# Gate and up projections of the second block: 512 weight columns moving against activations held, and the product turned by TensorE

## The reference, cut to what matters

```python
# x: (1, 256, 2048); h: (1, 256, 2048)
h = rms_norm_2(x, g_pre_ffn[l]) * (1.0 + scale_f) + shift_f
# w_ffn_gate, w_ffn_up: (2048, 5632); w_ffn_down: (5632, 2048)
f = (jax.nn.silu(h @ w_ffn_gate[l]) * (h @ w_ffn_up[l])) @ w_ffn_down[l]
x = x + gate_f * rms_norm_2(f, g_post_ffn[l])
```

## Time and profile before

| | |
|---|---|
| median of three runs | 2501.56 us |
| lowest and highest | 2496.78, 2502.04 us |
| profiled execution, its own time | 2500.57 us |
| its span in the profile | 2498.7 us |
| mean granted TensorE clock | 0.965 of full speed |
| PE busy | 2359.4 us (94%) |
| DVE busy | 1603.2 us (64%) |
| ACT busy | 1109.9 us (44%) |
| DMA | 502.02 MB, mean 201 GB/s |

### The profile page before, as it was taken

How to read it: one execution, slowest core, us unless ns; L and a number is a source line. 1 busy time by engine, 2 the same in 40 slices (tenths; PEclk the granted TensorE clock), 3 DMA queues, 4 the chain that set the end, 5 groups by cost and what they waited for, 6 DMA issues and landing times.

```text
span 2498.7 us, 37713 instructions
## 1 busy us (share of the span) xinstructions
PE 2359.4 (94%) x15624; PEld 2121.9 (85%) x15624; DVE 1603.2 (64%) x2266; ACT 1109.9 (44%) x1725; POOL 23.3 (1%) x59
## 2 busy tenths in 40 slices
PE   6989899899999999999979999996999999999997
PEld 5879777689998899998858787675999988999985
DVE  3996656678887778888765464646555555545444
ACT  3423566444444334444445464544434444444442
POOL 0000000000000000000000000000000000000000
PEclk9989989989999999999989899997999999999998
DMA  7745412668888888888854453252666667655552
GB/s 184 245 138 168 131 51 76 219 211 276 277 275 285 310 279 279 272 287 290 297 166 147 146 186 109 85 173 102 212 225 214 226 232 222 222 177 186 186 193 76
DMA packets 137770, 502.02 MB, mean 201 GB/s; under 512 B 15312, under 2 KB 15312, under 8 KB 137344
## 3 DMA queue, kind: packets, MB, share of 16 engines
q1 hardware_dynamic: 136368, 494.37, 58.6%
q0 software_dynamic: 1232, 5.24, 1.3%
HBM read 494.31 MB, written 5.24 MB: 200 GB/s over the span
## 4 chain that ended last, share of the span: by engine, by line
PE 84%; DVE 10%; ACT 3%; DMA 1%; issue 1%; POOL 1%; SPq 0%; ACTq 0%; DVEq 0%
PE bank L573 77%; DVE conv_y L1535 3%; DVE w_lo L1462 3%; PE bank L722 1%; DMA raw<-weights 1%; PE bank L757 1%; PE bank L545 1%; ACT w_hi L1034 1%; PE bank L610 0%; PE bank L739 0%; DVE wide L1480 0%; PE bank L622 0%; PE bank L752 0%; DVE x L1994 0%; DVE wide L1992 0%
## 5 line engine op out<-in xcount | busy, mean ns | idle before, releaser
L1462 DVE TENSOR_TENSOR w_lo<-raw,w_hi 128x1024 fp32r<-128x1024 f32 x737 | 888.0, 1220 | 550.6 <-ACT w_hi L1034 550.3
L573 PE MATMUL bank<-h_hi,w_hi 128*128 128x256 f32 x3472 | 993.7, 286 | 21.0 <-DVE w_lo L1462 20.6
L1034 ACT ACTIVATE w_hi<-raw 128x1024 fp32r<-128x1024 f32 x737 | 759.8, 1052 | 522.2 <-PE bank L573 503.4
L573 PE MATMUL bank<-h_lo,w_hi 128*128 128x256 f32 x3472 | 986.9, 284 | 0.0
L573 PE MATMUL bank<-h_hi,w_lo 128*128 128x256 f32 x3472 | 986.7, 284 | 0.0
L573 PEld LDWEIGHTS bank<-h_hi,w_hi 128*128 128x128 f32 x3472 | 670.1, 193 | 31.8 <-DVE w_lo L1462 30.9
L573 PEld LDWEIGHTS bank<-h_lo,w_hi 128*128 128x128 f32 x3472 | 670.4, 193 | 0.1
L573 PEld LDWEIGHTS bank<-h_hi,w_lo 128*128 128x128 f32 x3472 | 669.9, 193 | 0.0
L573 PE MATMUL bank<-w_hi,ff_hi 128*128 128x512 f32 x704 | 276.0, 392 | 2.9 <-DVE w_lo L1462 2.9
L573 PE MATMUL bank<-w_lo,ff_hi 128*128 128x512 f32 x704 | 274.0, 389 | 0.0
L573 PE MATMUL bank<-w_hi,ff_lo 128*128 128x512 f32 x704 | 274.0, 389 | 0.0
(11 more groups left out here) (293 smaller groups left out, 1818.1 us busy)
## 6 DMA issues: line engine op xcount, KB each, us to landing
raw<-weights SPq DMA_DIRECT2D x924, 512.0 KB, 4.4
bias_rows<-table POOLq DMA_DIRECT2D x1, 3072.0 KB, 35.5
raw<-weights SPq DMA_DIRECT2D x5, 504.0 KB, 3.4
x<-x SPq DMA_DIRECT2D x2, 1024.0 KB, 5.8
bias<-bias_rows POOLq DMA_DIRECT2D x1, 2048.0 KB, 17.1
out<-x SPq DMA_DIRECT2D x8, 256.0 KB, 2.0
lasting<-params SPq DMA_DIRECT2D x1, 550.0 KB, 7.7
raw<-weights SPq DMA_DIRECT2D x1, 488.0 KB, 3.2
```

The lines of the kernel that those rows point to most:

```text
L573: t = e.matmul(out, s, m, start=opens and first and q == 0, stop=closes and last and q == 2)
L1034: e.activation(w_hi[:, n % PART_SLOTS, 0:widths[i]], raw[:, i % RAW_SLOTS, 0:widths[i]], ACT.Copy).then_inc(hi_ready, 1)
L1462: e.tensor_tensor(w_lo[:, slot, 0:widths[i]], raw[:, i % RAW_SLOTS, 0:widths[i]], w_hi[:, slot, 0:widths[i]].bitcast(F32), ALU.subtract).t ...
```

## The change

Gate and up of the second block go from the tile form to the group form. The 22 tiles of a half become six groups: five of 512 columns and one of 256. The product is then tokens on partitions; it is held in one buffer `product` of 2 x 512 columns, and TensorE transposes it 128 x 128 at a time into banks 6 and 7, two feature tiles (a "pair", one bank) together. ScalarE rounds the turned pair from the bank into `ff_hi`, VectorE makes `ff_lo` from the bank. The transposes of a group are put behind the first weight chunk of the next gate group, or, for the last group of a half, behind the first chunk of the first down group. The order of the weights in memory follows the plan; the number of weight chunks and of ada chunks stays. The diff below has, in this order, the plan and the buffer, then TensorE's program, ScalarE's and VectorE's.

```diff
+FF_GROUPS = [[(6 * half + g, P * FF_HALF * half + 512 * g, min(512, P * FF_HALF - 512 * g)) for g in range(6)] for half in range(2)]
...
-        for j in range(FF_HALF * half, FF_HALF * (half + 1)):
-            p.project(("gate", j), "w_ffn_gate", P * j, P)
-            p.project(("up", j), "w_ffn_up", P * j, P)
+        for g, col, n in FF_GROUPS[half]:
+            p.project(("gate", g), "w_ffn_gate", col, n)
+            p.project(("up", g), "w_ffn_up", col, n)
...
-        sw_g = place("sw_g", FR, 2048, [P, 2, T])
+        product = place("product", FR, 2048, [P, TT, 512])
...
+        def ff_pairs(g):
+            half, at_group = divmod(g, 6)
+            return range(11 * half + 2 * at_group, min(11 * half + 2 * at_group + 2, 11 * (half + 1)))
...
+            def turn_product(g):
+                for pair in ff_pairs(g):
+                    b = 6 + pair % 2
+                    fill(b)
+                    for at_tile in range(2):
+                        col = (2 * (pair - ff_pairs(g)[0]) + at_tile) * P
+                        for tt in range(TT):
+                            w.wait_ge(ffn_product, FF_TILES + 2 * g + tt + 1)
+                            t = e.transpose(banks[b][:, at_tile * T + tt * P:at_tile * T + (tt + 1) * P], product[:, tt, col:col + P], identity)
+                    t.then_inc(ff_turned, 1)
+                    free[b] = ff_ready, FF_TILES + pair + 1
...
-                    tile(("gate", j), h_hi, h_lo, need, (ffn_silu, FF_TILES + j + 1))
-                    tile(("up", j), h_hi, h_lo, need, (ffn_product, FF_TILES + j + 1))
+                for g, col, n in FF_GROUPS[half]:
+                    gating = group_steps(("gate", g), n, (0, 1), h_hi, h_lo, need)
+                    next(gating)
+                    if g % 6:
+                        turn_product(g - 1)
+                    whole(gating)
+                    free[0], free[1] = (ffn_silu, FF_TILES + 2 * g + 1), (ffn_silu, FF_TILES + 2 * g + 2)
+                    group(("up", g), n, (2, 3), h_hi, h_lo, need)
+                    free[2], free[3] = (ffn_product, FF_TILES + 2 * g + 1), (ffn_product, FF_TILES + 2 * g + 2)
+                ff_need = lambda k, half=half: w.wait_ge(ff_ready, FF_TILES + 11 * half + k // 2 + 1)
...
+                    down = group_steps(("down2", half, n), 512, pair, ff_hi, ff_lo, ff_need)
+                    next(down)
+                    if n == 0:
+                        turn_product(6 * half + 5)
+                    whole(down)
...
+            def ff_round(g, first_chunk):
+                round_until(first_chunk + AHEAD)
+                for pair in ff_pairs(g):
+                    w.wait_ge(ff_turned, pair + 1)
+                    jj = 2 * (pair % 11)
+                    e.activation(ff_hi[:, jj:jj + 2, :].rearrange("p a t -> p (a t)"), banks[6 + pair % 2][:, :], ACT.Copy).then_inc(ff_rounded, 1)
...
+                for g, col, n in FF_GROUPS[half]:
+                    if g % 6:
+                        ff_round(g - 1, groups["gate", g][0][0])
+                    outs = made(("gate", g))
+                    if g:
+                        w.wait_ge(ff_turned, ff_pairs(g - 1)[-1] + 1)
+                    for tt in range(TT):
+                        e.activation(product[:, tt, 0:n], outs[tt][:, 0:n], ACT.Silu).then_inc(ffn_silu, 1)
+                    round_until(final["up", g] + AHEAD)
+                ff_round(6 * half + 5, groups["down2", half, 0][0][0])
...
+            def ff_rest(g, first_chunk):
+                rests_until(first_chunk + AHEAD)
+                for pair in ff_pairs(g):
+                    w.wait_ge(ff_rounded, FF_TILES + pair + 1)
+                    jj = 2 * (pair % 11)
+                    hi, lo = (which[:, jj:jj + 2, :].rearrange("p a t -> p (a t)") for which in (ff_hi, ff_lo))
+                    e.tensor_tensor(lo, banks[6 + pair % 2][:, :], hi.bitcast(F32), ALU.subtract).then_inc(ff_ready, 1)
...
+                for g, col, n in FF_GROUPS[half]:
+                    if g % 6:
+                        ff_rest(g - 1, groups["gate", g][0][0])
+                    rests_until(final["gate", g] + AHEAD)
+                    outs = made(("up", g))
+                    for tt in range(TT):
+                        w.wait_ge(ffn_silu, FF_TILES + 2 * g + tt + 1)
+                        e.tensor_tensor(product[:, tt, 0:n], outs[tt][:, 0:n], product[:, tt, 0:n], ALU.mult).then_inc(ffn_product, 1)
+                ff_rest(6 * half + 5, groups["down2", half, 0][0][0])
```

More of the change, by code:

```diff
@@ L492, in two_blocks @@
         m_scored, m_taken, m_maxed, m_exped, m_weighted = sem("m_scored"), sem("m_taken"), sem("m_maxed"), sem("m_exped"), sem("m_weighted")
+        ff_turned = sem("ff_turned")
         m_turned, m_T_ready, m_made, mla_rounded, mla_ready = sem("m_turned"), sem("m_T_ready"), sem("m_made"), sem("mla_rounded"), sem("mla_ready")
@@ L1005, in tensor_program @@
             need = h_need(3)
-            for half in range(2):
-                for j in range(FF_HALF * half, FF_HALF * (half + 1)):
-                    tile(("gate", j), h_hi, h_lo, need, (ffn_silu, FF_TILES + j + 1))
-                    tile(("up", j), h_hi, h_lo, need, (ffn_product, FF_TILES + j + 1))
-                ff_need = lambda k, half=half: w.wait_ge(ff_ready, FF_TILES + FF_HALF * half + k + 1)
+            def turn_product(g):
[9 more added lines that the diff above has]
+                    free[b] = ff_ready, FF_TILES + pair + 1
+            for half in range(2):
+                for g, col, n in FF_GROUPS[half]:
[8 more added lines that the diff above has]
+                ff_need = lambda k, half=half: w.wait_ge(ff_ready, FF_TILES + 11 * half + k // 2 + 1)
                 for n in range(4):
@@ L1014, in tensor_program @@
                     pair = (2 * (n % 2), 2 * (n % 2) + 1)
-                    group(("down2", half, n), 512, pair, ff_hi, ff_lo, ff_need)
+                    down = group_steps(("down2", half, n), 512, pair, ff_hi, ff_lo, ff_need)
[3 more added lines that the diff above has]
+                    whole(down)
                     if half:
```

## The result

The changed kernel took 2478.72 us (median of four runs, 2478.00 to 2479.82), beside 2499.87 us for the kernel before (median of four, three of them those shown above and one more). Later series of the same two kernels gave 0.9926 (0.9914 to 0.9939) and 0.9942 (0.9927 to 0.9958), with medians of the changed kernel, 2481.2 and 2480.76, at that low end. Over all 15 runs of the one and 57 of the other the means are 2480.7 and 2498.0, 17.3 us apart; each kernel by itself spreads over 8 to 12 us. Every ratio here is against runs of the kernel before in the same series.

A forecast was written before the change was run, and what follows sets the result against it. From 1722 to 2475 us the bound was how closely TensorE starts its matmuls. Matmuls save 25.5 us, transposes and switches add 12.9, so 12.6 less than 2500.57: 2488.0 us, range 2481 to 2498.

The forecast's parts named there:

- the term for the transposes: 88 transposes added to TensorE's order in gate/up and down stages: 10.6 us plus 2.3 for changes of kind, 12.9 together.
- the base: Profiled execution of the kernel before, 2500.57 us, from which 12.6 us were taken with no correction for scatter.
- The matmuls: Gate/up stages: pairs of 256 columns made into one of 512 give back 0.0133 us each, 25.5 us for both halves.
- its 0.2 us: Start of the first gate/up half at granted clock 0.50, where no gain is known: worth 0.2 us, left in the sum.
- the switch: PE's change of kind into and out of each of 12 transpose bursts: 0.19 us for both sides, 2.3 us in all.
- The sign: Whole-kernel time below 2482 us would make the prediction wrong, with the transposes hidden.
- its lower bounds: Low end of the transpose and switch costs in the stages, 9.7 and 0.1 us: 15.7 us less, 2484.9 us.
- A: At the bursts, transposes cost their full records, 0.272 us each: 26.2 against 25.5, 2501 us, no change; chance 0.07.
- B: VectorE's product comes late, PE stops 1.3 us at each of 12 bursts: 2503.6 us, 2496 with half hit; chance 0.09.
- C: Granted clock falls behind the transpose bursts, 3 us each, 36 us for all 12: 2524 us; chance 0.03.
- D: In gate/up, one matmul of 512 columns costs as much as two of 256, or nearly: 2513.5 us; chance 0.02.
- VectorE's hold: Behind transposes VectorE waits for ScalarE's copies before `w_lo`: hold of 2.5 us, second `ff_lo` near 5.5 us, hidden.

## Why the prediction was wrong

The direction, the mechanism on TensorE and what hides what were right. The size was off: the step that failed is the term for the transposes, 12.9 us where they cost 10.0, and beside it the base from which the sum was taken. Of the 9.3 us between 2488.0 and 2478.72, the transposes are 2.9, the base 2.6, the luck of the first four runs 2.0, and 1.7 stay open.

**The matmuls** were forecast at 25.5 us, 12.8 for a half. Measured without transposes: 12.7. The fixed part of 13 ns for each matmul, read from two stages, carried over to h as the held operand, as the earlier trace rows said. It belongs to the full clock. At the start of the first gate/up stage, before and after, with the granted clock at 0.50, 24 steps of 256 columns and 12 steps of 512 take the same 5.12 us, 0.2133 and 0.4267 each:

```profile
1722.51 0.42 PE L573 MATMUL bank<-h_hi,w_lo 128*128 128x256 f32 x1
1727.63 0.41 PE L573 MATMUL bank<-h_hi,w_lo 128*128 128x256 f32 x1
```

```profile
1716.55 0.63 PE L579 MATMUL bank<-w_lo,h_hi 128*128 128x512 f32 x1
1721.67 0.63 PE L579 MATMUL bank<-w_lo,h_hi 128*128 128x512 f32 x1
```

```profile
1717.00:1722.00 5.00, 5.00 (x13) 3.94 (x12) 2.97 (x4) 0.46 (x1) 0.00 (x0) 0.50 0.94 306
```

There the change gives nothing, as the prediction suspected for its 0.2 us. What the 13 ns consist of isn't shown.

**The transposes** are the term of the sum that was mis-sized: "10.6 + 2.3 = 12.9 us". They cost 2 x (4.5 + 0.5) = 10.0, so the stages should give 15.5, which is 2 x (8.25 - 0.50) by the two windows that hold no stretch at the lower clock. Of the 2.9 us too much, 1.8 are the price of a transpose (88 at 0.12 instead of 0.10) and 1.1 the switch (12 at 0.19 instead of 0.10). In the price I stood between 0.11 and 0.13 and should have taken the lower row: the earlier trace rows has it behind matmuls of 512 columns, as here, while the earlier trace rows has four at another place, behind two small matmuls; why those start further apart isn't shown. In the switch I took 0.19 from two fp32 matmuls with partial operands. Its way back was right (0.33 there, 0.32 here, where 0.227 is the pace), but the way in costs nothing, as the earlier trace rows already showed.

The first pair of profiles gave 16.6, because in the last down stage the kernel before has a stretch at the lower clock (0.72 over 2446 to 2452 us, and six fp32 matmuls for the last norm in 4.38 us where the changed kernel's first profile has 3.22) that the changed one has not. Over three profiles before and four after, the whole way from the first gate matmul to the last on `ff_lo` is 758.1 and 742.5, 15.6 less.

**The sign** "below 2482, where the transposes would have been hidden" read the low side wrongly: the time is below 2482, and the transposes are paid in full, 10.0 us.

**The base.** I wrote "This execution is 1.0 us under the median of the three runs, 2501.56, and the runs spread over 5 us, so I put no correction for it", and took three runs over 5 us as the scatter. 57 runs of that kernel lie between 2493.13 and 2504.89 us with a mean of 2498.0, 2.6 under the execution that I started from. Four runs of the changed one within 1.8 us, 2.0 under the mean of its 15, were luck. For the scatter below its lower bounds, 2484.9, the range had 3.9 us. From the mean of 2498.0 the same sum with the measured transposes gives 2482.5, inside the range. Against the difference of the means of all runs, 17.3 us, the stages leave 1.7. With standard deviations of 2.3 and 2.4 us the difference of the means is uncertain by 1.3 us either way, so 1.7 is a little outside. That 1.3 may be too small, for series by series the difference is 20.8, 18.0, 15.1 (one run) and 14.7; whether a part of the 1.7 belongs to the changed program stays open.

**One wait was left out.** The earlier trace rows and the prediction have one wait of PE between 1721 and 2483 us. The view of that window has a second, in the last down stage:

```profile
PE bank L622 <- DVE diag L1503: 2.4, 1, 2.4
```

It is the same in both kernels and changes nothing in the sum, but the end isn't set by TensorE's pace alone all the way to 2475 us.

**The rivals.** A fell: starts 0.099 apart, with records of 0.272. The 275 ns that the Trainium skill, "TensorE: Matmul & The Clock Gate", section "PE-mode transpose", gives for a transpose are met as the length of a record and not as a pace. B fell as forecast, with its lead of 1.2 us met to the tenth; the kernel without the chunk ahead shows what a late product costs, 16.6 us. C fell: the clock is 1.00 in the burst, and still with bursts of sixteen and with waits of up to 0.9 us. D fell: with 960 matmuls of 512 columns in it, the second gate/up stage without transposes took 242.48 us, where the forecast is 240.7 and 1.8 for the ada sum. The formula that the prediction takes for D from the Trainium skill, "TensorE: Matmul & The Clock Gate", section "Back-to-back issue gap", is given there for the isolated gap of a single matmul; the streams here start 120.0 and 226.7 ns apart. VectorE's hold was over at 1767.8, 5.3 us behind the group's end where 5.5 were worked out, and behind the bursts TensorE never waits for `w_lo`.

## What to carry to other kernels

Where the fp32r matmuls of this kernel start one behind the other with no wait and at a granted clock of 1.00, the gap between starts has a part that doesn't depend on the width (13 ns, at 120 ns for 256 columns and 227 for 512), and twice the width buys it back. At 0.50 there is nothing to buy back. A new layout that it takes must be paid from that: here a feature tile saves 48 x 0.0133 = 0.64 us over gate and up together, and its two transposes cost 0.2; with one projection for each turned tile it would be 0.32 against 0.2, and where the group is no wider than the tile it is a loss. Price such an insertion by the distance of starts in a row that stands among the same neighbours, put it one piece of work behind its producer, and judge an effect of 1 to 16 us by windows over stages without a stretch at the lower clock, which repeat to 0.02 us, since a window that holds such a stretch moves by 1 to 2 us and the times of single executions spread over 8 to 12.

## What was not expected of the hardware

One and the same program reaches a fixed point of its course 5.2 us apart in two executions (1721.48 and 1716.25), and between two profiles the granted clock differs in stretches where TensorE works with gaps. The fixed 13 ns between starts, present at the full clock, are gone at 0.50. Sixteen transposes in a row run at 0.104 us each (1771.02 to 1772.69, the starts of the first and of the matmul behind) at a granted clock of 1.00 in the stage.
